# Attention by pairs of heads, and a new spread of the adaLN slots, in a two-layer encoder

## The chip, the cores and the metric

One core of a Trainium2 chip runs the whole program. The metric is the device time of one execution in microseconds (us); lower is better. Before the change the median of three runs is 1363.38 us (1358.85 to 1363.46).

## What is computed

Two sequences of 256 tokens (512 rows together) of width 1024 pass two encoder layers in fp32. A layer has two kinds of attention heads that read the same normalised input. Group A has 8 query heads of width 64 over 2 key/value heads, with a norm on each query and key and rotary positions. Group B has 8 heads whose queries (64 + 32 rotary columns) and keys/values are expanded from low-rank latents. Cut to what matters:

```python
mod = silu(c) @ w_ada[l] + b_ada[l]            # six vectors: shift/scale/gate, twice
h = rms_norm(x, g_attn) * (1 + scale_a) + shift_a
q_a, k_a, v_a, c_q, c_kv, k_r = split(h @ w_in)
o_a = softmax(rope(norm(q_a)) @ rope(norm(k_a)).T * 64**-0.5) @ v_a
q_b = rms_norm(c_q) @ w_uq                     # query expansion, 8 heads x 96
k_nope, v_b = split(rms_norm(c_kv) @ w_ukv)    # key/value expansion, 8 heads x (64 + 64)
o_b = softmax([q_b] @ [k_nope, rope(k_r)].T * 96**-0.5) @ v_b
x = x + gate_a * (concat(norm(o_a), norm(o_b)) @ w_o)
val, gate = split(conv3(norm_mod(x) @ w_up))
x = x + gate_f * ((silu(gate) * val) @ w_down)
```

## The kernel before, in words

The kernel writes each engine's program by hand; semaphores are the only order between engines. Weights come in **slots** of 128 x 1024 through a ring of four: SyncE (SP) loads a slot, ScalarE (ACT) rounds it to `w_hi` (L818), GpSimd (POOL) makes the rest `w_lo` (L446), and TensorE (PE) makes each product of three matmuls, hi x hi, hi x lo, lo x hi (`product`, L497 to L503). All matmul outputs lie in PSUM, eight banks of 512 columns.

Of `w_ada` all but the first vector is worked off on VectorE (DVE) in 88 **adaLN slots** of 128 x 1024: each is multiplied with silu(c) of either sequence and summed (`ada_slot`, L1038, both inputs in SBUF; or `ada_half_slot`, L1065, where half of silu(c) lies in PSUM, for vectors numbered `HALVED` and above). `ada_plan` is a table that says behind which step DVE takes a slot; `ADA_BEHIND` sets behind which weight slot SP queues its load.

A layer runs in these stages:

1. norm, then the input projection in five column chunks; DVE norms and rotates queries and keys (`QK_BLOCKS`, ends with L1237);
2. query expansion: 4 slots, each 4 row tiles x 2 x 3 matmuls of 192 columns; ACT copies the results to `qb` (L906); then key/value expansion: 2 slots, matmuls of 512 columns, copied to `kb` and `vb` (L913, L916);
3. attention over 32 **units** (`UNITS`), one head of one sequence each. For unit i PE transposes queries (and keys) into a bank (L663, L666, L667), ACT copies them out (`qa_t` L937, `qk_t` L939), PE makes the scores (L685), DVE takes the maximum (L1259) and its negative (L1262), ACT makes the exponentials with their sums (L949), PE transposes them (L693, two units late), DVE copies them out (L1268) and inverts the sum (L1269), PE multiplies with the values (L709, three units late), DVE divides (L1279). During the first scores PE runs 40 throw-away matmuls (`WARM_UP`, `keep_warm` L509). Between units DVE takes adaLN slots, 13 in layer 0 and none in layer 1;
4. transposes of the outputs (L540), output projection `w_o`, 8 tiles (`out_tile`), update of x (L1157) and its squares (L1144);
5. norm, then FFN in three groups of 8, 8 and 6 up tiles (ACT L993, DVE taps L1321, ACT silu L997, a_hi L999, DVE a_lo L1334) and 8 down tiles each.

`take` in `plan_banks` counts the uses of a bank, `wait_free` and `wait_full` are waits on them. POOL's rotation of `qb` and copy of the rotary keys (L466 to L475) come between two splits and end with `b_ready`.

## Time and profile before

| | us |
|---|---|
| median of 3 runs (lowest, highest) | 1363.38 (1358.85, 1363.46) |
| the profiled execution | 1359.79 |
| its span, first to last instruction | 1357.9 |
| mean granted TensorE clock | 0.959 |
| busy: PE, PE weight load | 1233.1 (91%), 1040.1 (77%) |
| busy: DVE, ACT, POOL | 819.2 (60%), 565.8 (42%), 470.1 (35%) |

A matmul's time is modelled from its start to its end and neighbours overlap, so a busy PE is not PE at its peak. Times of instructions below count from the start of the span. The program is long and its stages have different limits, so it is read stage by stage: the stage borders used are the start of the first query expansion, of the first scores, of the first `w_o` product, and of the sums for the next norm.

### The profile page before, as it was taken

Reading aid. Unit: us, or ns where it says so; the run is one execution under the profiler, and the core shown is the slowest. Engines: PE = TensorE matmul, PEld = TensorE weight load, DVE = VectorE, ACT = ScalarE, POOL = GpSimd, SP = SyncE. Lnnn points to the kernel's source line nnn. Section 1 sums busy time; section 2 is a strip of 40 time slices with the busy share of each in tenths; the row PEclk is TensorE's granted clock in tenths of the full one; section 3 lists DMA queues with packets and bytes.
Section 4 is the critical chain, followed back from the end, with each engine's and each line's share of the span. In section 5 each row is a group of like instructions: output and inputs, shape, how many; then the busy total and the mean of one; then the engine's idle time right before and its main releaser. Section 6 shows DMA issues by size and latency. Waiting matters only on the chain.

```text
span 1357.9 us, 19350 instructions
## 1 busy us (share of the span) xinstructions
PE 1233.1 (91%) x6424; PEld 1040.1 (77%) x6424; DVE 819.2 (60%) x1641; ACT 565.8 (42%) x1041; POOL 470.1 (35%) x224
## 2 busy tenths in 40 slices
PE   4798887795999999899978999999899999999996
PEld 0697776674788887778757998887778888888885
DVE  5668578777766667866865584764466513321444
ACT  1844445522644234223335546663454314432451
POOL 0244400032244433352453455003234543453452
PEclk9897979997999999899989989999999999999998
DMA  9433222033244634554542232001133331332221
GB/s 375 157 123 113 90 78 69 26 109 124 78 150 153 212 130 161 179 196 152 172 153 78 79 107 65 1 1 63 63 109 124 110 108 62 101 120 89 92 94 62
DMA packets 42748, 153.68 MB, mean 113 GB/s; under 512 B 4912, under 2 KB 5424, under 8 KB 42288
## 3 DMA queue, kind: packets, MB, share of 16 engines
q1 hardware_dynamic: 42672, 152.72, 32.7%
q8 instruction: 41, 0.67, 0.2%
q14 instruction: 35, 0.29, 0.1%
HBM read 150.61 MB, written 2.10 MB: 112 GB/s over the span
## 4 chain that ended last, share of the span: by engine, by line
issue 62%; POOLq 34%; PE 2%; POOL 1%; DVE 0%; DMA 0%; DVEq 0%; ACT 0%; SPq 0%; ACTq 0%
POOLq L447 33%; PE ps L497 1%; PE ps L503 1%; PE ps L498 1%; POOL qb_tmp L466 0%; POOL qb L471 0%; POOLq L452 0%; DMA c_all<-c_rows 0%; POOLq L476 0%; DVE x L1356 0%; POOLq L445 0%; POOLq L448 0%; PE ps L528 0%; POOL kb L473 0%; PE ps L523 0%
## 5 line engine op out<-in xcount | busy, mean ns | idle before, releaser
L446 POOL TENSOR_TENSOR w_lo<-w_raw,w_hi 128x1024 fp32r<-128x1024 f32 x184 | 450.0, 2446 | 859.7 <-ACT w_hi L818 835.3
L497 PE MATMUL ps<-h_hi,w_hi 128*128 128x512 f32 x832 | 329.8, 396 | 16.6 <-POOLq L448 7.9
L498 PE MATMUL ps<-h_lo,w_hi 128*128 128x512 f32 x832 | 325.6, 391 | 0.0
L503 PE MATMUL ps<-h_hi,w_lo 128*128 128x512 f32 x832 | 325.4, 391 | 0.0
L818 ACT CAST w_hi<-w_raw 128x1024 fp32r<-128x1024 f32 x184 | 187.2, 1047 | 140.6 <-PE ps L497 140.2
L1321 DVE SCALAR_TENSOR_TENSOR u_sb<-ps,par,u_sb 128x510 f32<-128x510 f32 x176 | 131.8, 749 | 122.6 <-ACT u_sb L993 110.1
L497 PEld LDWEIGHTS ps<-h_hi,w_hi 128*128 128x128 f32 x832 | 157.2, 189 | 61.9 <-issue 14.7
L503 PEld LDWEIGHTS ps<-h_hi,w_lo 128*128 128x128 f32 x832 | 157.2, 189 | 33.0
L498 PEld LDWEIGHTS ps<-h_lo,w_hi 128*128 128x128 f32 x832 | 157.4, 189 | 31.6
L1065 DVE SCALAR_TENSOR_TENSOR ada_prod<-ada_raw,ps 128x512 f32<-128x512 f32 x224 | 144.9, 684 | 8.6 <-issue 0.9
L497 PE MATMUL ps<-a_hi,w_hi 128*128 128x512 f32 x352 | 139.3, 396 | 11.0 <-DVEq L1159 7.5
L498 PE MATMUL ps<-a_lo,w_hi 128*128 128x512 f32 x352 | 138.6, 394 | 0.0
L503 PE MATMUL ps<-a_hi,w_lo 128*128 128x512 f32 x352 | 138.5, 394 | 0.0
L1157 DVE SCALAR_TENSOR_TENSOR x<-ps,mod,x 128x256 f32<-128x256 f32 x128 | 56.1, 480 | 136.1 <-PE ps L503 134.1
L993 ACT ACTIVATE u_sb<-ps,par 128x512 f32<-128x512 f32 x88 | 67.7, 775 | 146.8 <-PE ps L503 146.8
L1038 DVE SCALAR_TENSOR_TENSOR ada_prod<-ada_raw,c_all 128x1024 f32<-128x1024 f32 x64 | 92.4, 1443 | 8.7 <-DMA ada_raw<-ada_slots 3.7
L949 ACT ACTIVATE prob<-ps,nmx 128x256 f32<-128x256 f32 x128 | 59.5, 469 | 82.5 <-DVE nmx L1262 79.8
L497 PE MATMUL ps<-w_hi,h_hi 128*128 128x256 f32 (+1 forms) x320 | 91.3, 285 | 0.4 <-DVE h_lo L1109 0.3
L498 PE MATMUL ps<-w_lo,h_hi 128*128 128x256 f32 (+1 forms) x320 | 90.0, 281 | 0.0
L503 PE MATMUL ps<-w_hi,h_lo 128*128 128x256 f32 (+1 forms) x320 | 89.9, 281 | 0.0
L497 PEld LDWEIGHTS ps<-a_hi,w_hi 128*128 128x128 f32 x352 | 67.1, 191 | 28.0 <-POOLq L448 7.3
L997 ACT ACTIVATE sil<-u_sb 128x512 f32<-128x512 f32 x44 | 27.8, 633 | 126.6 <-DVEq L1326 126.6
(129 smaller groups left out, 1713.8 us busy)
## 6 DMA issues: line engine op xcount, KB each, us to landing
w_raw<-w_slots SPq DMA_DIRECT2D x184, 512.0 KB, 3.5
ada_raw<-ada_slots SPq DMA_DIRECT2D x88, 512.0 KB, 4.5
shift<-shift_slots SPq DMA_DIRECT2D x2, 2048.0 KB, 12.1
x<-x_t SPq DMA_DIRECT2D x2, 1024.0 KB, 12.8
y_t<-x SPq DMA_DIRECT2D x8, 256.0 KB, 2.2
c_all<-c_rows SPq DMA_DIRECT2D x1, 1024.0 KB, 5.1
par<-params SPq DMA_DIRECT2D x1, 251.0 KB, 10.7
tab<-tables SPq DMA_DIRECT2D x1, 192.0 KB, 10.0
```

Of the source, the lines that this page charges most:

```text
L446: nc.gpsimd.tensor_tensor(w_lo[:, j, :], w_raw[:, j, :], w_hi[:, j, :].bitcast(F32), ALU.subtract)
L447: nc.gpsimd.drain()
L497: hh = mm(out, stat[0], mov[0], start=first, stop=False)
L498: hl = mm(out, stat[0], mov[1], start=False, stop=False)
L503: return mm(out, stat[1], mov[0], start=False, stop=last)
L818: nc.scalar.copy(w_hi[:, j, :], w_raw[:, j, :]).then_inc(hi_done, 1)
L949: A(prob[:, i % 3, q, :], ps[:, i % 3, q * SEQ:(q + 1) * SEQ], ACT.Exp, bias=nmx[:, i, q:q + 1], scale=d ** -0.5, accum_out=sme[:, i, q:q ...
L993: A(u_sb[:, e, half, :], ps[:, bank(key), :], ACT.Identity, bias=par[:, L, bass.ds(ft + PC_CB, 1)], scale=par[:, L, bass.ds(ft + (PC_CW + ...
L1038: V.scalar_tensor_tensor(out=ada_prod[:], in0=ada_raw[:, j % 4, :], scalar=1.0, in1=c_all[:, s, :], op0=ALU.mult, op1=ALU.mult, accum_out= ...
L1065: V.scalar_tensor_tensor(out=ada_prod[:, 512 * s:512 * s + 512], in0=ada_raw[:, q % 4, 512 * t:512 * t + 512], scalar=1.0, in1=ps[:, 6 + s ...
L1157: V.scalar_tensor_tensor(out=xs, in0=ps[:, bank(key), c], scalar=gate, in1=xs, op0=ALU.mult, op1=ALU.add)
L1321: V.scalar_tensor_tensor(out=u3[:, :, dst:dst + SEQ - 1], in0=p3[:, :, src:src + SEQ - 1], scalar=par[:, L, bass.ds(at + (PC_CW + tap * 2 ...
```

## The change

- **Expansions.** Query heads are expanded by fours: 2 slots with matmuls of 384 columns in place of 4 with 192. Keys and values share one slot. Their expansion no longer stands ahead of the attention: the keys' half stands before the first scores and the values' half behind them. The warm-up matmuls of the attention go; those of the norms stay. A layer has 89 weight slots, not 92.
- **Pairs.** 32 units become 16 pairs: for group A heads p and p + 4, for group B heads h and h + 1, of one sequence. Scores of a pair fill two banks (two sets), one DVE instruction takes the negative maxima of both heads, ACT makes four exponentials without sums, ACT (not DVE) copies the transposed pair out in one instruction, and a column of ones behind the values (`va`, `vb`, 65 columns a head) gives the sums in the product with the values. The softmax scale moves into the query norm's weights and into the copy of `qb`. The exponentials are transposed one pair late, the values come two pairs late.
- **adaLN slots.** Layer 0: attention 13 to 16, `w_o` 8 to 5, FFN 48 to 40 (up tiles of the second group 15 to 11, of the third 11 to 7; up tiles with two slots go from 12 to 4). Layer 1: attention 0 to 8, up tiles of the first group 8 as before. Which vectors go in halves follows from that.

```diff
-S_UKV = S_UQ + 4
-S_WO = S_UKV + 2
+S_UKV = S_UQ + 2
+S_WO = S_UKV + 1
+PAIRS = [("a", s, (p, p + 4)) for s in range(NSEQ) for p in range(4)]
+PAIRS += [("b", s, (h, h + 1)) for s in range(NSEQ) for h in range(0, HEADS, 2)]
+S_BANK, PT_BANK, QT_BANK, O_BANK = (0, 2), 4, 6, 7
-HALVED = 4
+HALVED = (4, 5, 6, 7, 8, 10)
...
-    plan += [(("unit", i), S_WO - 1, 1) for i in range(1, 26, 2)]
-    plan += [(("wo", m), S_WO + m, 1) for m in range(KD)]
-    ups = [[1] * 8, [2, 2, 2, 2, 2, 2, 2, 1], [2, 2, 2, 2, 2, 1]]
+    plan += [(("unit", i), S_WO - 1, 1) for i in range(1, NP + 1)]
+    plan += [(("wo", m), S_WO + m, 1) for m in range(1, 6)]
+    ups = [[1] * 8, [1, 2, 1, 2, 1, 2, 1, 1], [2, 1, 1, 1, 1, 1]]
+    plan += [((1, "unit", i), SLOTS + S_WO - 1, 1) for i in range(1, KD + 1)]
...
-WARM_UP = {-1: 14, 0: 12, 1: 8, 2: 6}
-STATS_AT_UNIT = {12: (0, 0), 20: (0, 1), 28: (1, 0)}
+STATS_AT_STEP = {6: (0, 0), 10: (0, 1), 14: (1, 0)}
...
+                def expand_kv(s):
+                    j = slot(L, S_UKV)
+                    pe.wait_ge(ct_ready, 3 * L + 3)
                     for t in range(TT):
+                        key = ("ukv", s, t)
+                        wait_free(pe, L, key)
+                        product(ps[:, bank(key), :], [r[:, 2, t * P:t * P + P] for r in (ct_hi, ct_lo)],
+                                [r[:, j, s * 512:s * 512 + 512] for r in (w_hi, w_lo)], True, True,
...
+                def fill(j, part):
+                    pe.wait_ge(qt_ready, n)
...
+                def scores(j):
+                    pe.wait_ge(qt_ready, FILLS * L + fills_before(j + 1))
...
+                        pe.wait_ge(exp_ready, 4 * (NP * L + j - 1))
...
+                def prob_transposes(j):
+                    pe.wait_ge(pt_ready, NP * L + j)
+                    for u in range(2):
                         for q in range(2):
+                            pe.wait_ge(exp_ready, 4 * (NP * L + j) + 2 * u + q + 1)
...
+                def outputs(j):
+                    pe.wait_ge(o_done, NP * L + j)
+                    pe.wait_ge(pt_ready, NP * L + j + 1)
...
+                for i in range(-1, NP + 2):
+                    if i + 1 < NP:
+                        fill(i + 1, 0)
+                    if i == -1:
+                        expand_kv(0)
+                    if 0 <= i < NP:
+                        scores(i)
+                    if i == 0:
+                        expand_kv(1)
+                    if i + 1 < NP and PAIRS[i + 1][0] == "b":
+                        fill(i + 1, 1)
+                    if 0 <= i - 1 < NP:
+                        prob_transposes(i - 1)
+                    if 0 <= i - 2 < NP:
+                        outputs(i - 2)
+                    if i >= NP:
+                        for k in range(2):
+                            output_transposes(L, 2 * (i - NP) + k)
...
+                for i in range(-1, NP + 1):
+                    if i + 1 < NP:
+                        if i + 1 >= 2:
+                            act.wait_ge(s_full, NP * L + i)
+                        take_fill(i + 1, 0)
+                    if i + 1 < NP and PAIRS[i + 1][0] == "b":
+                        take_fill(i + 1, 1)
+                    if 0 <= i - 1 < NP:
+                        j = i - 1
+                        act.wait_ge(pt_full, NP * L + j + 1)
...
+                        nc.scalar.copy(prob_t[:, j % 2, :, :, :],
+                                       ps[:, PT_BANK:PT_BANK + 2, :].rearrange("p u (k q) -> p u k q", k=2)
+                                       ).then_inc(pt_ready, 1)
...
+                    if 0 <= i < NP:
+                        act.wait_ge(max_ready, NP * L + i + 1)
+                        for c in range(4):
+                            A(prob[:, i % 2, c, :], ps[:, S_BANK[i % 2] + c // 2, (c % 2) * SEQ:(c % 2 + 1) * SEQ],
+                              ACT.Exp, bias=nmx[:, i, c:c + 1]).then_inc(exp_ready, 1)
...
+                for k in range(KD // 2):
                     output_hi(L, k)
+                act.wait_ge(o_done, NP * (L + 1))
                 stats(1, 1)
...
+                for i in range(NP + 2):
+                    if i < NP:
+                        b = S_BANK[i % 2]
+                        dve.wait_ge(s_full, NP * L + i + 1)
+                        V.tensor_reduce(out=nmx[:, i, :], in_=ps[:, b:b + 2, :].rearrange("p u (q k) -> p (u q) k", q=2),
+                                        op=ALU.max, axis=AX_X, negate=True).then_inc(max_ready, 1)
...
+                        V.reciprocal(r4, o4[:, :, :, HD:VW])
...
+                            V.tensor_tensor(o_sb[:, 2 * s:2 * s + 2, col:col + HD], o4[:, u, :, 0:HD],
+                                            r4[:, u].broadcast_to([P, 2, HD]), ALU.mult)
```

How the rows stand on PE at the start of the attention of layer 0 (`proj` holds queries and keys of group A, `prob` the exponentials). Before, from the key transposes on:

```order
L652 MATMUL ps<-ident,proj 128x128 x4
L663 MATMUL ps<-ident,proj 128x128 x2
L509 MATMUL ps<-ones 128x128 x26
L685 MATMUL ps<-ka_t,qa_t 128x256 x2
L663 MATMUL ps<-ident,proj 128x128 x2
L509 MATMUL ps<-ones 128x128 x8
L685 MATMUL ps<-ka_t,qa_t 128x256 x2
L509 MATMUL ps<-ones 128x128 x6
```

Now, from the end of the values' expansion on:

```order
L517 MATMUL ps<-w_hi,ct_lo 128x512
L680 MATMUL ps<-ident,proj 128x128 x2
L708 MATMUL ps<-ka_t,qk_t 128x256 x4
L722 MATMUL ps<-ident,prob 128x128 x8
L680 MATMUL ps<-ident,proj 128x128 x2
L708 MATMUL ps<-ka_t,qk_t 128x256 x4
L722 MATMUL ps<-ident,prob 128x128 x8
L738 MATMUL ps<-va,prob_t 128x65 x8
```

The throw-away matmuls are gone, and one row now holds the scores, transposes or value products of two heads; a pair has as many matmuls as two units had.

On DVE in the attention of layer 0, one unit with a slot before, and what follows it:

```order
L1259 TENSOR_REDUCE mx<-ps 128x2
L1262 TENSOR_SCALAR nmx<-mx 128x2
L1268 COPY prob_t<-ps 128x512
L1269 RECIPROCAL rin<-sme 128x2
L1279 TENSOR_TENSOR o_sb<-ps,rin 128x2x64
L1038 SCALAR_TENSOR_TENSOR ada_prod,mod<-ada_raw,c_all 128x1024 x2
```

Now, a whole pair between two slots:

```order
L1101 SCALAR_TENSOR_TENSOR ada_prod,mod<-ada_raw,c_all 128x1024 x2
L1324 TENSOR_REDUCE nmx<-ps 128x4
L1332 RECIPROCAL rin<-ps 128x4
L1336 TENSOR_TENSOR o_sb<-ps,rin 128x2x64 x2
L1101 SCALAR_TENSOR_TENSOR ada_prod,mod<-ada_raw,c_all 128x1024 x2
```

The copies of the transposed exponentials and the negations have left DVE, and a slot comes with every pair instead of with every second unit.

On DVE at the end of the output projection of layer 0, before, from the update of x for the last tile to the reciprocal of the next norm:

```order
L1157 SCALAR_TENSOR_TENSOR x<-ps,mod,x 128x256 x2
L1144 TENSOR_TENSOR ssum<-ssum,sq_x 128x512
L1038 SCALAR_TENSOR_TENSOR ada_prod,mod<-ada_raw,c_all 128x1024 x2
L1080 TENSOR_TENSOR mod<-mod,par 128x16
L1084 TENSOR_SCALAR mod<-mod 128x16
L1086 TENSOR_TENSOR mod<-mod,par 128x16
L1144 TENSOR_TENSOR ssum<-ssum,sq_x 128x512
L1094 RECIPROCAL rstd<-root 128x4
```

Now, from the last slot (behind tile 5) to the same reciprocal:

```order
L1101 SCALAR_TENSOR_TENSOR ada_prod,mod<-ada_raw,c_all 128x1024 x2
L1143 TENSOR_TENSOR mod<-mod,par 128x16
L1147 TENSOR_SCALAR mod<-mod 128x16
L1149 TENSOR_TENSOR mod<-mod,par 128x16
L1220 SCALAR_TENSOR_TENSOR x<-ps,mod,x 128x256 x2
L1207 TENSOR_TENSOR ssum<-ssum,sq_x 128x512
L1220 SCALAR_TENSOR_TENSOR x<-ps,mod,x 128x256 x2
L1207 TENSOR_TENSOR ssum<-ssum,sq_x 128x512 x2
L1157 RECIPROCAL rstd<-root 128x4
```

The slot and the finishing of its vector have moved from between the last update of x and the norm to two tiles ahead of it.

## Rows read from the trace of the kernel before

**Rows 1.** Windows between stage borders: borders, length, busy time (count) by engine, clock, DMA.

```profile
117.14:147.06 29.92, 28.03 (x179) 26.81 (x180) 13.54 (x21) 18.05 (x37) 21.51 (x18) 0.79 0.45 159
147.06:264.38 117.32, 94.22 (x636) 83.87 (x635) 93.21 (x221) 57.17 (x178) 5.39 (x7) 0.93 0.18 59
264.38:331.71 67.33, 49.46 (x211) 38.26 (x209) 53.05 (x72) 17.74 (x27) 21.47 (x8) 0.89 0.35 118
331.71:731.59 399.88, 378.59 (x1628) 308.22 (x1628) 273.56 (x620) 147.12 (x193) 164.72 (x68) 0.97 0.45 154
801.70:827.12 25.42, 25.42 (x175) 24.21 (x174) 10.38 (x17) 18.04 (x37) 20.77 (x16) 0.87 0.45 146
827.12:918.25 91.13, 85.62 (x637) 78.92 (x635) 63.87 (x167) 57.18 (x178) 6.16 (x9) 0.98 0.01 1
918.25:971.47 53.22, 47.06 (x212) 37.28 (x210) 20.89 (x37) 17.73 (x27) 19.25 (x8) 1.00 0.24 80
971.47:1345.18 373.71, 368.71 (x1629) 302.96 (x1629) 159.90 (x276) 144.36 (x190) 156.32 (x65) 1.00 0.28 92
```

**Rows 2.** Waits of PE, 147 to 262 us: us in total, times, longest.

```profile
PE ps L693 <- DVEq L1270: 18.2, 12, 2.2
PE ps L685 <- ACTq L941: 4.9, 4, 2.4
```

**Rows 3.** Waits of PE, 332 to 745 us: us in total, times, longest.

```profile
PE ps L523 <- DVEq L1146: 15.5, 2, 12.7
PE ps L497 <- POOLq L448: 9.8, 7, 3.8
PE ps L497 <- DVEq L1159: 7.5, 3, 5.7
```

**Rows 4.** Timeline of DVE at the end of L1237: start, us.

```profile
129.22 2.60 DVE L1237 TENSOR_TENSOR proj<-proj,st_qk 128x512 f32<-128x512 f32 x1
810.04 2.61 DVE L1237 TENSOR_TENSOR proj<-proj,st_qk 128x512 f32<-128x512 f32 x1
```

**Rows 5.** Timeline of PE in layer 1: scores of neighbouring units, group A (two apart), group B.

```profile
843.92 1.03 PE L685 MATMUL ps<-ka_t,qa_t 128*128 128x256 f32 x4
848.49 1.03 PE L685 MATMUL ps<-ka_t,qa_t 128*128 128x256 f32 x4
...
902.32 1.03 PE L685 MATMUL ps<-qk_t 96*128 96x256 f32 x4
904.90 1.03 PE L685 MATMUL ps<-qk_t 96*128 96x256 f32 x4
```

**Rows 6.** Groups by line, engine and shape: busy us, mean ns, idle before.

```profile
L1214 DVE TENSOR_REDUCE st_qk<-sq_qk 128x16 f32<-128x1024 f32 x4 | 4.9, 1221 | 1.0 <-ACT sq_qk L886 0.8
L1269 DVE RECIPROCAL rin<-sme 128x2 f32<-128x2 f32 x64 | 9.9, 155 | 0.0
L1279 DVE TENSOR_TENSOR o_sb<-ps,rin 128x128 f32<-128x128 f32 x64 | 18.7, 292 | 16.5 <-issue 12.3 <-PE ps L709 4.2
L949 ACT ACTIVATE prob<-ps,nmx 128x256 f32<-128x256 f32 x128 | 59.5, 469 | 82.5 <-DVE nmx L1262 79.8 <-issue 2.6
L818 ACT CAST w_hi<-w_raw 128x1024 fp32r<-128x1024 f32 x184 | 187.2, 1047 | 140.6 <-PE ps L497 140.2 <-issue 0.3
L939 ACT COPY qk_t<-ps 96x512 f32<-96x512 f32 x32 | 18.6, 580 | 7.8 <-issue 6.0 <-PE ps L667 1.5
```

**Rows 7.** Timeline of DVE in the attention of layer 0: a slot, and the next unit's maximum.

```profile
210.97 1.22 DVE L1038 SCALAR_TENSOR_TENSOR ada_prod<-ada_raw,c_all 128x1024 f32<-128x1024 f32 x1
...
213.63 0.69 DVE L1259 TENSOR_REDUCE mx<-ps 128x2 f32<-128x512 f32 x1
```

**Rows 8.** Timeline of DVE in the output projection of layer 0: two updates of x, half a slot.

```profile
305.68 0.88 DVE L1157 SCALAR_TENSOR_TENSOR x<-ps,mod,x 128x256 f32<-128x256 f32 x2
...
308.91 3.24 DVE L1038 SCALAR_TENSOR_TENSOR ada_prod<-ada_raw,c_all 128x1024 f32<-128x1024 f32 x1
...
312.29 0.88 DVE L1157 SCALAR_TENSOR_TENSOR x<-ps,mod,x 128x256 f32<-128x256 f32 x2
```

More of the change, by code:

```diff
@@ L82 @@
 SLOTS = _at
-ROUNDS = SLOTS // RING
-assert SLOTS % RING == 0 and sum(GROUPS) == FT
+assert sum(GROUPS) == FT
 PC_GATTN = 0
@@ L177, in plan_banks @@
         take(("lat", j), 4 + j)
-    for s in range(4):
+    for s in range(2):
         for t in range(TT):
@@ L182, in plan_banks @@
         for t in range(TT):
-            take(("ukv", s, t), t)
+            take(("ukv", s, t), 4 + t % 2)
     take("kat", 7)
-    pairs = 0
-    for i in range(-1, NU + LAG_O):
-        if i + 1 < NU and UNITS[i + 1][3]:
-            take(("qt", i + 1), 4 + pairs % 2)
-            pairs += 1
-        if 0 <= i < NU:
-            take(("s", i), i % 3)
-        if 0 <= i - LAG_P < NU:
-            take(("pt", i - LAG_P), 3)
-        if 0 <= i - LAG_O < NU:
-            take(("o", i - LAG_O), 6 + (i - LAG_O) % 2)
     for k in range(KD):
@@ L262, in encoder_kernel @@
         kr_rot = put("kr_rot", [P, TT, ROT])
+        at_cg = base[0]
         cg = put("cg", [P, 2, 2, HD])
@@ L626, in _ @@
                             last.then_inc(full[t], 1)
-                width = 2 * QK_B
-                for s in range(4):
+                width = 4 * QK_B
+                for s in range(2):
                     j = slot(L, S_UQ + s)
@@ new lines, in scores @@
+                def scores(j):
+                    group, s, heads = PAIRS[j]
+                    pe.wait_ge(qt_ready, FILLS * L + fills_before(j + 1))
+                    if j == 0:
+                        pe.wait_ge(ka_ready, L + 1)
+                    if j < 2:
+                        for t in range(S_BANK[j], S_BANK[j] + 2):
+                            key = ("uq", 1, t)
+                            pe.wait_ge(free[bank(key)], n_use(L, key) + 1)
+                    else:
+                        pe.wait_ge(exp_ready, 4 * (NP * L + j - 1))
+                    for u in range(2):
@@ new lines, in scores @@
+                    last.then_inc(s_full, 1)
+                def prob_transposes(j):
+                    if j == 0:
+                        for t in range(2, TT):
+                            key = ("ukv", 1, t)
+                            pe.wait_ge(free[bank(key)], n_use(L, key) + 1)
+                    pe.wait_ge(pt_ready, NP * L + j)
+                    for u in range(2):
+                        for q in range(2):
+                            pe.wait_ge(exp_ready, 4 * (NP * L + j) + 2 * u + q + 1)
+                            for k in range(2):
+                                last = nc.tensor.transpose(ps[:, PT_BANK + u, k * SEQ + q * P:k * SEQ + q * P + P],
+                                                           prob[:, j % 2, 2 * u + q, k * P:k * P + P], ident[:])
+                    last.then_inc(pt_full, 1)
@@ L712, in _ @@
-                    if i >= NU:
-                        output_transposes(L, i - NU)
-                for k in range(LAG_O, KD // 2):
-                    output_transposes(L, k)
+                                v = va[:, 2 * s + k, u, :] if group == "a" else vb[:, 2 * s + k, heads[u], :]
+                                c = (2 * u + q) * VW
+                                last = mm(ps[:, O_BANK, c:c + VW], prob_t[:, j % 2, u, k, q * P:q * P + P], v,
+                                          start=(k == 0), stop=(k == 1))
@@ new lines, in outputs @@
+                    last.then_inc(o_full, 1)
+                for i in range(-1, NP + 2):
[14 more added lines that the diff above has]
+                    if i >= NP:
+                        for k in range(2):
+                            output_transposes(L, 2 * (i - NP) + k)
@@ L1415, in _pack @@
     halved = ada.reshape(-1, KD // 2, 2, P, 2, SLOT // 2).transpose(0, 4, 1, 3, 2, 5).copy()
-    for n in range(HALVED, len(ORDER)):
+    for n in HALVED:
         for q in range(KD):
```

346 lines of the change are left out of this document (148 added, 198 removed).

## The prediction

> **What bounds the kernel now.** I read the windows between stage borders first, because a share over the whole span mixes stages with different limits, then PE's waits in the stages where PE has idle time, then the instructions behind those waits. The layers do the same work except for adaLN slots, so the same stage of the other layer is the best yardstick. Three things are to be seen [rows 1]:
>
> - Attention, first scores to first `w_o` product, takes 117.3 us in layer 0 and 91.1 in layer 1. In layer 1 PE is busy 85.6 of 91.1; it is the limit there. In layer 0 PE is busy only 94.2 of 117.3 and DVE 93.2. PE waits 18.2 us for bank 3, which DVE frees late (L1270), and 4.9 for the query copies of ACT [rows 2]; the clock falls to 0.93. This stage waits on DVE with its 13 slots.
> - The output projection takes 67.3 us in layer 0 and 53.2 in layer 1. PE waits 12.7 us once for the sums of the norm [rows 3], which DVE ends behind 8 slots.
> - The FFN takes 399.9 us in layer 0 (48 slots) and 373.7 in layer 1 (8 slots). Waits of 9.8 us for splits and 7.5 for banks [rows 3] are layer 0's.
>
> Between the norm's sums and the first expansion I expect no difference, and none in the prologue.
>
> **Part 1: expansions ahead of the attention.** The stage from the first query expansion to the first scores takes 29.9 and 25.4 us with PE hardly idle [rows 1]. Now the key transposes need the query expansion and DVE's norm of the keys. The latter ends at 131.8 and 812.7 us [rows 4], 14.7 us after the first expansion in layer 0 and 11.0 in layer 1. The expansion is 48 matmuls of 384 columns, 18432 columns: 15.4 us at 1.2 GHz and 7.7 at 2.4. PE starts it at 1.2 GHz after a pause (granted 0.79 and 0.87 in these windows, and 1.00 later [rows 1]). So layer 0 waits for DVE, 14.7 us; in layer 1 the expansion ends last or nearly so, 12.3. From there to the first scores PE has 8 transposes and the keys' expansion, 12 matmuls of 512 columns: 7168 columns or 3.0 us at 2.4 GHz. ACT must have copied `ka_t`, the first queries and a first bank of keys meanwhile, so some 1.6 us of waiting: 4.6 (bounds 3.0, and 9 if ACT's copies lie bare). The stage becomes 19.3 and 16.9 us: **-10.6 and -8.5**. The 40 warm-up matmuls a layer are inside this sum and the next.
>
> What comes along costs nothing on the path. Three weight slots a layer less is 3 x 1.05 us less on ACT [rows 6], with as many splits and loads. The copy of the values in two pieces, one scaling of the query weights and four small memsets on POOL lie beside PE; POOL's rotation (`b_ready`) is needed only at pair 8, some 30 us later. On SP 16 loads now queue behind weight slot `S_WO` + 6 and hold the next one until the attention is over; that slot is needed at the last `w_o` tile, over 35 us later.
>
> **Part 2: pairs.** PE's work in a pair is that of two units. At full clock neighbouring units start 2.58 us apart in group B and two units 4.57 us apart in group A [rows 5], so a pair costs 5.16 and 4.57, and 16 pairs 8 x 9.73 = 77.8 us. One more column for each head is noise. The values' expansion adds 6144 columns, 2.6 us: PE needs 80.4.
>
> DVE per pair: maximum over 1024 columns 1.22, reciprocal 0.16, two products 0.58 [rows 6] and a slot, 2.66 from its start to the next instruction [rows 7]: 4.62 and some drains, about 4.8. That is under 5.16 and a little over 4.57. ACT per pair in group B: four exponentials of at most 0.47, two fills of 0.58 and one copy of 1024 columns, at most 1.05 (nearest row L818) [rows 6]: 4.1. In group A it is less. No engine is above PE's 77.8 by much, so PE should be the limit with slots or without.
>
> Waits remain, since each engine is in order. ACT's copy of `prob_t` now stands ahead of the next exponentials and waits for PE; PE's next `fill` waits until ACT has emptied the one bank for queries, and scores queue behind it; three times ACT squares outputs between pairs; at the end the last pair's maximum, exponentials, copy and products lie bare. The bounds are none, and the 23.1 us that PE idles in layer 0's old stage (5.5 in layer 1) [rows 1]. I take 5.3 for layer 1, near its old 5.5, and 8.5 for layer 0, as its slots fill DVE. With 2.3 us from the last product over the division to the first `w_o` product, the stage takes 80.4 + 8.5 + 2.4 = 91.3 in layer 0, **-26.0**, and 80.4 + 5.3 + 2.3 = 88.0 in layer 1, **-3.1**.
>
> **Part 3: output projection.** In layer 1 PE idles 6.2 of 53.2 us [rows 1]. Part of it is the fourth output tile, whose remainder on DVE stood behind the norm of group B; now the first four all come before it. I take **-2.6** (bounds 0 and -6.2). In layer 0 DVE needs 6.61 us per tile with a slot, 3.24 of it one half that runs beside a split on POOL [rows 8], and a PE tile of 24 x 512 columns takes 5.1. Eight such tiles are 12.7 us late at the norm; five slots, behind tiles 1 to 5, put DVE up to 7.5 late, and two tiles without slots (under 2 us each) give most of it back. So layer 0 comes to layer 1's 50.6 and half a us more: 67.3 to 51.1, **-16.2**.
>
> **Part 4: FFN of layer 0.** It is 26.2 us longer than layer 1's, and layer 1 takes 8 single slots without loss. Up tiles with two slots go from 12 to 4 and no two are neighbours; by their number alone 26.2 x 8/12 = 17 us come back. Lateness also no longer adds up from tile to tile, so I take **-20** (bounds -4 and -26).
>
> **Sum.** 10.6 + 8.5 + 26.0 + 3.1 + 2.6 + 16.2 + 20 = 87.0 us. Against the profiled execution, 1359.8 us (span 1357.9), that is 1272.8. The profiled one lies 3.6 under the median, so I round up: **1275 us**.
>
> **Rivals.**
>
> - *Exchange between ACT and PE sets the pair.* With exponentials at 0.47 apiece, ACT does 1.9 of exponentials and 0.8 of the first fill, PE fills again (0.4) and transposes (0.9), ACT copies (1.05); with half a us for semaphores 5.5 us a pair in group B, 5.0 in group A: 84 a layer and not 77.8, or 13 us in both, 1288; if ACT's squares all lie bare as well, 1294. For it: one bank for fills. Against: before, PE waited only 4.9 us for fills. Chance 0.15.
> - *Slots and POOL in each other's way.* A slot in the attention takes 2.66 us [rows 7], but half a slot beside a split on POOL took 3.24 instead of 1.22 [rows 8]. Pairs 1 to 3 now run while POOL still splits one slot and rotates `qb`. Two us for the split and up to 0.5 for each other half make 4 us a layer on DVE, of which PE feels most in group A: 1282. Chance 0.1. The Trainium skill, SBUF — State Buffer, "Who interferes with whom", states it as a rule: a DVE instruction with two SBUF inputs contends with a GpSimd instruction that reads SBUF, and the later one waits in full. By that rule, vector 9, which goes from halves in PSUM to whole slots, loses a protection too. The trace agrees with the rule in the 3.24 against 1.22.
> - *The FFN keeps its waits.* Lateness there runs from taps over silu and cast to the next split, so a single two-slot tile may still hold PE. Then 4 us come back and not 20: 1291. Chance 0.1.
> - *Slower.* The matmuls that fell away kept PE busy. If PE ran at 1.2 GHz through both attentions, its 80.4 us would double: 161 less the waits it would cover (14), 1275 + 147 = 1422. It decides from more than half of the stage at the low level: 88 us of gain against 2 x 80.4. Against it: layer 1 held 0.98 with the same mixture, and layer 0 held 0.93 with 20% idle [rows 1]. Chance 0.04.
>
> **How the numbers follow.** The forecast has 0.61, with 1262 to 1286 by its own bounds (nothing waits in the attention, all 26 come back; or 3 us more in each of four stages). The first three rivals lie between 1282 and 1294, and two of them together give 1306. The range is 1260 to 1306. About 0.5% (7 us) is what a measurement tells from no change. All cases but the last are faster by far more: faster 0.96, same 0.01, slower 0.03.
>
> **What would show it.** Right: first scores some 10 and 8 us sooner; distances between scores of 5.2 us in group B and 4.6 to 4.9 in group A at clock 1.00 in both layers; PE's wait for the norm sums in layer 0 near 3 us instead of 12.7; both FFNs within 8 us of each other. Wrong: distances over 5.5 us, waits of PE for ACT at each fill (exchange) or of DVE for POOL (slots); a clock under 0.9 in the attention; FFN waits for splits near 10 us as before. A total above 1306 would mean that pairs are slower than two units.

## The result, and the profile after

The change makes the kernel faster: 1291.69 us median (1291.19 to 1293.44) against 1362.26 for the kernel before in the same session, ratio 0.9488 (95% interval 0.9467 to 0.9509). That is 70.6 us; 87 were forecast. The time lies inside the range of 1260 to 1306, but outside the forecast's own bounds of 1262 to 1286, among the times of the rivals. The profiled execution took 1291.37 us, its span 1289.3, at a mean granted clock of 0.971.

The windows between the same stage borders in the changed kernel answer to [rows 1] (borders, length, busy time and count by engine, clock, DMA), with expansions, attention, projection and FFN of layer 0, then of layer 1:

```profile
117.01:136.19 19.18, 15.53 (x69) 14.01 (x70) 13.57 (x21) 11.00 (x21) 7.46 (x3) 0.85 0.38 138
136.19:234.77 98.58, 88.85 (x618) 81.16 (x617) 72.93 (x137) 68.88 (x140) 16.09 (x22) 0.95 0.28 88
234.77:292.15 57.38, 47.94 (x209) 37.05 (x209) 46.24 (x60) 15.82 (x23) 20.32 (x8) 0.98 0.36 118
292.15:674.27 382.12, 371.95 (x1629) 306.43 (x1629) 255.18 (x552) 147.66 (x193) 163.82 (x68) 0.98 0.44 150
743.88:760.42 16.54, 14.20 (x68) 12.98 (x69) 11.15 (x17) 11.22 (x21) 7.51 (x3) 0.90 0.30 97
760.42:852.12 91.70, 85.90 (x619) 78.64 (x617) 53.19 (x104) 67.76 (x138) 16.09 (x22) 0.98 0.16 53
852.12:902.81 50.69, 47.39 (x208) 37.19 (x208) 21.23 (x37) 16.43 (x25) 19.22 (x8) 1.00 0.26 84
902.81:1276.51 373.70, 368.72 (x1629) 302.98 (x1629) 160.13 (x276) 144.37 (x190) 156.30 (x65) 1.00 0.28 92
```

| stage, us | before | forecast | after | off by |
|---|---|---|---|---|
| expansions, layer 0 / 1 | 29.9 / 25.4 | 19.3 / 16.9 | 19.2 / 16.5 | -0.1 / -0.4 |
| attention, layer 0 / 1 | 117.3 / 91.1 | 91.3 / 88.0 | 98.6 / 91.7 | +7.3 / +3.7 |
| output projection, layer 0 / 1 | 67.3 / 53.2 | 51.1 / 50.6 | 57.4 / 50.7 | +6.3 / +0.1 |
| FFN, layer 0 / 1 | 399.9 / 373.7 | 379.9 / 373.7 | 382.1 / 373.7 | +2.2 / 0 |

So nearly all that is missing lies in the two attentions (11.0 us) and in the output projection of layer 0 (6.3). One border of the kernel before was read wrong: the 801.70 of [rows 1] lies 0.7 us behind the start of layer 1's first query expansion, which is at 800.99, so that stage took 26.1 us and not 25.4.

The waits of PE from the first scores of layer 0 to the first query expansion of layer 1 (136 to 745 us; total, times, longest) answer to [rows 2, 3]:

```profile
PE ps L537 <- DVEq L1209: 10.4, 2, 7.2
PE ps L684 <- ACTq L988: 6.9, 3, 2.7
PE ps L511 <- DVEq L1222: 5.8, 3, 5.0
...
PE ps L722 <- ACT prob L1014: 1.1, 1, 1.1
PE ps L511 <- POOLq L461: 0.3, 1, 0.3
```

The 18.2 us for bank 3 are gone, and so are the FFN's waits for splits, 9.8 us before and 0.3 now. The wait for the norm's sums (L537) is 7.2 us, not near 3. The second line is most of what is left in the attention (4.9 us for query copies before): PE cannot refill the one query bank (L684) until ACT has emptied it (L988).

PE in the attention of layer 0, scores of neighbouring pairs (L708) and the longest waits, which answer to [rows 5] (start, length, instruction, idle time before):

```profile
148.74 1.89 PE L708 MATMUL ps<-ka_t,qk_t 128*128 128x256 f32 x8
...
153.31 1.89 PE L708 MATMUL ps<-ka_t,qk_t 128*128 128x256 f32 x8
...
171.79 0.31 PE L684 MATMUL ps<-ident,qb 128*96 128x128 f32 x1 [2.70 <-ACTq L988]
...
185.74 1.89 PE L708 MATMUL ps<-qk_t 96*128 96x256 f32 x8
...
190.95 1.89 PE L708 MATMUL ps<-qk_t 96*128 96x256 f32 x8
195.47 0.45 PE L684 MATMUL ps<-ident,qb 128*96 128x128 f32 x1 [2.62 <-ACTq L988]
...
202.22 3.15 PE L708 MATMUL ps<-qk_t 96*128 96x256 f32 x8
...
208.69 1.89 PE L708 MATMUL ps<-qk_t 96*128 96x256 f32 x8
```

Undisturbed pairs are 4.57 and 5.21 us apart, as forecast (4.57 and 5.16). But the scores at 202.22 come 11.27 us after those at 190.95. 2.62 us of the excess is a wait; the rest is the clock, as the windows of PE there show (PE's busy time, clock, DMA):

```profile
192.00:196.00 4.00, 1.38 (x7) 0.81 0.18 40
196.00:200.00 4.00, 4.00 (x21) 0.50 0.23 93
200.00:204.00 4.00, 4.00 (x17) 0.50 0.00 0
204.00:208.00 4.00, 4.00 (x31) 0.91 0.40 130
```

PE stood still for 2.6 us, and the granted clock then went to 0.50, the lower level. It costs 11.27 - 5.21 - 2.62 = 3.4 us in this distance and 6.47 - 5.21 = 1.3 in the next: 4.7. The same happens once in layer 1 (a wait of 2.22 at 819.04; distances of 9.28 and 5.53): 2.2 us.

What ACT did before the wait of 2.62 us in layer 0:

```profile
190.30 1.57 ACT L1014 ACTIVATE prob<-ps,nmx 128x256 f32<-128x256 f32 x4 [0.31 <-DVE nmx L1324]
191.74 0.65 ACT L872 ACTIVATE junk_o<-o_sb 128x512 f32<-128x512 f32 x1
...
192.55 0.63 ACT L872 ACTIVATE junk_o<-o_sb 128x512 f32<-128x512 f32 x1
...
193.33 1.28 ACT L878 ACT_TABLE_LOAD   x1
...
194.83 0.56 ACT L986 COPY qk_t<-ps 96x512 f32<-96x512 f32 x1
...
199.33 1.28 ACT L1014 ACT_TABLE_LOAD   x1
```

Behind pair 10 two squares (L872), the square root for the norm of group A (L878) and a load of the function table stand between the exponentials and the copy that frees the query bank; a second table load stands ahead of the next exponentials. The first wait (2.70) follows the squares behind pair 6, whose exponentials had also waited 1.61 us for a maximum that DVE made late. The third (1.62, at 217.41) has no squares ahead of it. There DVE takes a slot and its norm of group A (`NORM_A_AT`, four products) ahead of the maximum of pair 13, and the exponentials wait for it; DVE, then ACT:

```profile
212.25 1.68 DVE L1191 TENSOR_SCALAR o_sb<-o_sb,st_o 128x512 f32<-128x512 f32 x4
214.05 1.23 DVE L1324 TENSOR_REDUCE nmx<-ps 128x4 f32<-128x1024 f32 x1
...
215.31 1.57 ACT L1014 ACTIVATE prob<-ps,nmx 128x256 f32<-128x256 f32 x4 [2.37 <-DVE nmx L1324]
```

In the kernel before, the squares and the root stood in the attention too, and the root held PE there already. These are PE's scores behind its copy of queries, in layer 0 and in layer 1:

```profile
226.46 1.10 PE L685 MATMUL ps<-qk_t 96*128 96x256 f32 x4 [2.39 <-ACTq L941]
...
884.06 1.94 PE L685 MATMUL ps<-qk_t 96*128 96x256 f32 x4 [1.79 <-ACTq L941]
```

Undisturbed scores take 1.03 us [rows 5]. Behind the second of these waits they took 1.94, at a granted clock of 0.57 (884 to 888 us); behind the first the clock stayed at 1.00.

DVE in the output projection of layer 0 answers to [rows 8]:

```profile
264.96 0.88 DVE L1220 SCALAR_TENSOR_TENSOR x<-ps,mod,x 128x256 f32<-128x256 f32 x2
...
268.19 3.24 DVE L1101 SCALAR_TENSOR_TENSOR ada_prod<-ada_raw,c_all 128x1024 f32<-128x1024 f32 x1
...
271.57 0.88 DVE L1220 SCALAR_TENSOR_TENSOR x<-ps,mod,x 128x256 f32<-128x256 f32 x2
...
285.59 0.88 DVE L1220 SCALAR_TENSOR_TENSOR x<-ps,mod,x 128x256 f32<-128x256 f32 x2
...
288.59 3.38 DVE L1207 TENSOR_TENSOR ssum<-ssum,sq_x 128x512 f32<-128x512 f32 x2 [0.21 <-issue]
```

A tile with a slot still takes 6.61 us. The last output tile on PE ends at 284.9 (292.15 less the wait of 7.24), and only at 285.59 does DVE come to the update of the second last one. Of the last two sums of squares (the last row) one took 2.57 us and the other 0.69; the long one ran beside a split on POOL (288.27 to 290.61). Both of its inputs lie in SBUF.

### The profile page after: what moved, and what is told of

It reads as the page before. It is cut to its first block, busy times and chain, and to the rows that moved or that the text cites. A ratio compares the mean times of both kernels' runs of the same rounds, so it can differ in the third digit from the quotient of the medians.

```text
span 1289.3 us, 17964 instructions
## 1 busy us (share of the span) xinstructions
PE 1196.3 (93%) x6168; PEld 1009.3 (78%) x6168; DVE 764.4 (59%) x1416; ACT 572.3 (44%) x931; POOL 461.6 (36%) x227
## 4 chain that ended last, share of the span: by engine, by line
issue 60%; POOLq 35%; PE 2%; POOL 2%; DVE 1%; DMA 0%; DVEq 0%; ACT 0%; SPq 0%; ACTq 0%
POOLq L460 33%; PE ps L511 1%; PE ps L517 1%; PE ps L512 1%; POOL qb L485 1%; POOL kb L488 1%; POOLq L491 0%; POOL qb_tmp L480 0%; POOLq L466 0%; DMA c_all<-c_rows 0%; DVE x L1414 0%; POOLq L458 0%; POOLq L461 0%; PE ps L542 0%; PE ps L537 0%
## 5 line engine op out<-in xcount | busy, mean ns | idle before, releaser
L459 POOL TENSOR_TENSOR w_lo<-w_raw,w_hi 128x1024 fp32r<-128x1024 f32 x178 | 433.7, 2437 | 799.2 <-ACT w_hi L862 772.3
L862 ACT CAST w_hi<-w_raw 128x1024 fp32r<-128x1024 f32 x178 | 180.9, 1047 | 142.5 <-PE ps L511 142.2
L1128 DVE SCALAR_TENSOR_TENSOR ada_prod<-ada_raw,ps 128x512 f32<-128x512 f32 x192 | 124.2, 684 | 6.4
L1101 DVE SCALAR_TENSOR_TENSOR ada_prod<-ada_raw,c_all 128x1024 f32<-128x1024 f32 x80 | 111.8, 1397 | 10.9 <-DMA ada_raw<-ada_slots 3.6
L511 PE MATMUL ps<-w_hi,h_hi 128*128 128x256 f32 (+1 forms) x320 | 91.5, 286 | 0.1
L517 PEld LDWEIGHTS ps<-a_hi,w_lo 128*128 128x128 f32 x352 | 66.5, 189 | 14.0
L512 PEld LDWEIGHTS ps<-a_lo,w_hi 128*128 128x128 f32 x352 | 66.5, 189 | 13.7
```

The source lines that it names most:

```text
L459: nc.gpsimd.tensor_tensor(w_lo[:, j, :], w_raw[:, j, :], w_hi[:, j, :].bitcast(F32), ALU.subtract)
L511: hh = mm(out, stat[0], mov[0], start=first, stop=False)
L512: hl = mm(out, stat[0], mov[1], start=False, stop=False)
L517: return mm(out, stat[1], mov[0], start=False, stop=last)
L862: nc.scalar.copy(w_hi[:, j, :], w_raw[:, j, :]).then_inc(hi_done, 1)
L1101: V.scalar_tensor_tensor(out=ada_prod[:], in0=ada_raw[:, j % 4, :], scalar=1.0, in1=c_all[:, s, :], op0=ALU.mult, op1=ALU.mult, accum_out= ...
```

## Experiments

The theory after this reading: PE sets the pair, slots fit beside it, and the missing gain is ACT's squares with the root in the attention, and whole slots beside POOL's splits in the projection. The first rival is that the spread of the slots made the gain and pairs little; the second that slots hold up DVE in the attention whatever ACT does. All times are medians; ratios are against the kernel before on the same chip. The after kernel stands at 1291.69, 0.9488.

### Slots alone

The kernel before with the new table:

```diff
-    plan += [(("unit", i), S_WO - 1, 1) for i in range(1, 26, 2)]
-    plan += [(("wo", m), S_WO + m, 1) for m in range(KD)]
-    ups = [[1] * 8, [2, 2, 2, 2, 2, 2, 2, 1], [2, 2, 2, 2, 2, 1]]
+    plan += [(("unit", i), S_WO - 1, 1) for i in range(1, 33, 2)]
+    plan += [(("wo", m), S_WO + m, 1) for m in range(1, 6)]
+    ups = [[1] * 8, [1, 2, 1, 2, 1, 2, 1, 1], [2, 1, 1, 1, 1, 1]]
+    plan += [((1, "unit", i), SLOTS + S_WO - 1, 1) for i in range(1, 16, 2)]
```

> The kernel before with the new spread of the adaLN slots alone (16 behind units of layer 0, 5 behind output tiles, 40 in its FFN, 8 behind units of layer 1). Theory (units leave DVE no room, pairs do): output projection of layer 0 falls from 67.3 to about 57 us, its FFN from 400 to 382, but its attention grows by three slots of 2.66 us, 117 to 125, and layer 1's by some 4: 1346 us in all. Rival (the spread is what made the gain, pairs little): 1310 or less, with the attention of layer 0 no longer than 117.

Measured: 1361.38 us, ratio 0.9994 (0.9975 to 1.0013): no gain. Windows of attention, projection and FFN of layer 0, and of layer 1's attention:

```profile
147.56:268.66 121.10, 99.00 (x636) 86.50 (x635) 99.96 (x233) 57.16 (x178) 5.31 (x7) 0.89 0.21 70
268.66:329.55 60.89, 49.18 (x212) 38.26 (x210) 45.63 (x60) 17.72 (x27) 20.41 (x8) 0.94 0.32 106
329.55:708.37 378.82, 371.67 (x1629) 304.88 (x1629) 248.32 (x550) 147.37 (x193) 164.94 (x68) 0.99 0.43 151
805.35:915.29 109.94, 93.84 (x636) 84.19 (x635) 82.71 (x202) 57.17 (x178) 6.33 (x9) 0.92 0.12 39
```

Projection and FFN give 27.5 us, as expected, but eight slots among layer 1's units cost 18.8 us (91.1 to 109.9), 2.35 each, nearly their length, and layer 0's attention grew by 3.8. The expectation's "some 4" for layer 1 was wrong: between units there is next to no room. The rival falls: the spread by itself is worth nothing.

### Pairs alone

The changed kernel with the old table (13, 8 and 48 slots in layer 0, none in layer 1's attention; vector 9 in halves again), the lines above the other way round.

> The changed kernel with the old spread of slots (13 behind pairs of layer 0, 8 behind output tiles, 48 in its FFN, none in layer 1's attention). Theory: both attentions stay within 3 us of the changed kernel's 98.6 and 91.7, output projection of layer 0 goes back from 57.4 to about 67 and its FFN from 382 to 400: 1319 us. Rival (the spread is what freed the attention): the attention of layer 0 is back over 110 and the whole at 1335 or more.

Measured: 1310.18 us, ratio 0.9623 (0.9607 to 0.9639). Windows of the two attentions:

```profile
136.27:232.21 95.94, 87.38 (x619) 79.93 (x617) 65.61 (x125) 68.05 (x138) 16.09 (x22) 0.96 0.24 78
781.23:870.08 88.85, 84.22 (x618) 77.09 (x617) 33.01 (x71) 67.09 (x138) 12.42 (x22) 1.00 0.02 7
```

So pairs, with the expansions, give 52 us of the 70.6. No run has the expansions alone; by the stages some 20 of the 52 lie in them. The output projection took 63.3 (67 expected) and the FFN 398.7, whose waits for splits are back at 11.3 us. The spread gives 18.5 us on top of pairs and nothing clear of noise without: layer 1's attention takes eight slots for 2.85 us (88.85 to 91.70), 0.36 each, where units paid 2.35.

### No slots in the attention

```diff
-                    ada_at(L, ("unit", i))
+                    for _ in range(ADA_TAKES.get((L, "unit", i), 0)):
+                        n, q = taken[0] // KD, taken[0] % KD
+                        dve.wait_ge(ada_landed[q % 4], 16 * (2 * n + q // 4 + 1))
+                        dve.sem_inc(ada_used, 1)
...
+                        taken[0] += 1
```

> The changed kernel without DVE's multiplications of the 24 slots that stand in the two attentions (their vectors are left out of the computation; loads and order stay). Theory (a pair lasts as long as PE needs, slots fit beside it): distances between scores stay 4.56 and 5.21 us, only the last two pairs of layer 0, where a slot stands ahead of the last maximum and the last division, get shorter by 2 to 3 us: 1289. Rival (slots and POOL or PSUM readers get in each other's way): both attentions get shorter by 4 us or more, 1283 or less.

Measured: 1278.2 us, ratio 0.939 (0.9375 to 0.9406). The rival's number came, though layer 1 got shorter by 2.9 us and not by 4. Its two attentions:

```profile
136.49:225.37 88.88, 84.23 (x618) 77.10 (x617) 33.35 (x73) 67.12 (x138) 12.42 (x22) 1.00 0.30 101
750.32:839.17 88.85, 84.21 (x619) 77.08 (x617) 33.18 (x72) 67.10 (x138) 12.42 (x22) 1.00 0.17 54
```

Distances between undisturbed pairs stay at 4.57 and 5.21, so it is not POOL or PSUM that slots get in the way of. The waits for fills behind the squares of pairs 6 and 10 shrink from 2.70 and 2.62 to 0.80 and 2.22, the one behind DVE's norm (1.62) is gone, one of 0.57 stands behind the second table load, and the clock stays at 1.00. So 16 slots cost 9.7 us in layer 0 and 8 cost 2.85 in layer 1, not in the steady pairs but at those waits. This calls for the counterpart.

### No squares in the attention

```diff
-                        stats(g, s)
                         if (g, s) == (0, NSEQ - 1):
-                            group_root(0)
+                            act.sem_inc(o_root, 1)
```

> The changed kernel without ACT's squares and root between the pairs (the sums of squares of group A, and of the first sequence of group B, are left out of the computation; slots stay). Theory (neither slots nor squares hold PE by themselves, only a square behind a late maximum does): waits for fills under 1 us, clock at its upper level, attention 89 us in layer 0 and 87.5 in layer 1: 1278. Rival (slots alone make DVE late): the attention of layer 0 stays over 95: 1288 or more.

Measured: 1279.02 us, ratio 0.9385 (0.9367 to 0.9404). Its two attentions:

```profile
138.36:230.11 91.75, 86.98 (x618) 80.32 (x617) 72.90 (x137) 61.59 (x123) 16.08 (x22) 0.96 0.30 95
755.25:840.92 85.67, 83.88 (x618) 77.21 (x617) 53.13 (x104) 60.75 (x123) 16.08 (x22) 1.00 0.18 56
```

Layer 1, us in its attention: slots without squares 85.67, squares without slots 88.85, both 91.70. Eight slots by themselves leave PE 1.8 us of waits, so its own work is 83.9 us in a layer. Layer 0 came to 91.75, not 89: waits of 1.04, 1.60 and 1.06 us remain and the clock fell near its end, so 16 slots do cost something by themselves. The 1.60 is the wait behind DVE's norm of group A, unchanged, which confirms that squares have no part in it. In layer 0 the changed kernel lies 14.7 us over 83.9; without slots 9.7 come back, without squares 6.8, together more than there is (in layer 1 2.9 and 6.0 of 7.8). So a part of the cost belongs to both: squares behind a maximum that slots made late, and the clock that falls after a wait. The wait behind pair 6 in layer 0 shows it: 1.04 us with slots alone, 0.80 with squares alone, 2.70 with both. Neither single cause is enough. Without slots 88.9 us are left in either layer, 5.0 over PE's own work, and 3.6 of it are the waits of 0.80, 2.22 and 0.57 behind squares, root and table load.

### Values' expansion ahead of the scores

```diff
                     if i == -1:
                         expand_kv(0)
+                        expand_kv(1)
...
-                    if i == 0:
-                        expand_kv(1)
```

> The changed kernel with the values' half of the key/value expansion ahead of the first scores too, and no throw-away matmuls. Theory: first scores 2.6 us later and the attention as much shorter, but the first maximum (1.23) and the first exponentials (1.57) now have only one pair's scores beside them: PE waits some 3 us, 1295. Rival (the clock needs the matmuls there): the granted clock falls to its lower level after the first scores in both layers and each attention loses 5 us, 1302. Second rival (nothing hangs on the place): 1292.

Measured: 1299.5 us, ratio 0.9536 (0.9519 to 0.9552); 7.8 us slower than the change. The expansions became 4.0 and 3.4 us longer (23.2 and 19.9), and the attention did not become shorter (102.7 and 92.0). Without those 12 matmuls of 512 columns among the first scores new waits appear, 1.46 and 1.45 us for exponentials a few pairs later, and in layer 0 the stage's clock is 0.92 (0.95 in the change). In layer 1 it is 0.96 (0.98). The theory's direction held with too small a price; how much of it is the clock was not taken apart.

### The root at the end, and the squares one by one

The root behind the last exponentials, and with it DVE's norm of group A at the end and ahead of the slot there; then also one row tile of squares at a step:

```diff
-STATS_AT_STEP = {6: (0, 0), 10: (0, 1), 14: (1, 0)}
-NORM_A_AT = 12
+STATS_AT_STEP = {6: (0, 0), 7: (0, 1), 9: (0, 2), 10: (0, 3), 13: (1, 0), 14: (1, 1)}
+NORM_A_AT = NP
...
-                        if (g, s) == (0, NSEQ - 1):
-                            group_root(0)
+                    if i == NP - 1:
+                        group_root(0)
```

> The changed kernel with the square root for the norm of group A behind the last exponentials (it stands in the middle of them, behind pair 10, and brings two loads of ACT's function table of 1.28 us each), and DVE's norm of group A in the second last step. Theory (this root holds ACT back, PE's fills stand still for it and the clock falls): PE's waits for fills lose their longest one, the clock stays at its upper level in the second half, attention of layer 0 from 98.6 to 92 us and of layer 1 from 91.7 to 89: 1282. Rival (the squares, 1.7 us at a step, are enough to hold PE): under 2 us gained in each, 1289. Rival (the root now lies bare at the end): 1292 or more.

> As the run with the late root, and the squares of the outputs one row tile at a step (pairs 6, 7, 9, 10, 13, 14) in place of two at one step (6, 10, 14). Theory (what ACT does between two pairs is hidden as long as it is under a microsecond): no wait of PE for a fill over 1 us is left, attention 90 us in layer 0 and 87 in layer 1: 1278. Rival (six steps with 0.85 us wait as long together as three with 1.7): as the late root alone.

Measured: 1294.61 us, ratio 0.9501 (0.9463 to 0.954), and 1295.31, 0.9516 (0.9481 to 0.9551): neither is faster than the change. The waits inside did nearly what was expected: with both edits layer 0 has 1.90, 0.42 and 0.41 us where it had 2.70, 2.62 and 1.62 (the last of these went with DVE's norm, not with the squares). But at the end stands a new one; PE in the run with both (the first lies at the fill for pair 8, the last ahead of the output transposes):

```profile
171.86 0.32 PE L684 MATMUL ps<-ident,qb 128*96 128x128 f32 x1 [1.90 <-ACTq L988]
...
224.81 1.97 PE L554 MATMUL ps<-ident,o_sb 128*128 128x128 f32 x8 [2.93 <-DVEq L1192]
```

The transposes take 1.97 in place of 1.04 us: the clock has fallen again (0.50 from 226 to 230 us), and stays low into the output projection (clock 0.95 and 0.96 there in layers 0 and 1, 0.98 and 1.00 in the change). The attention took 95.0 and 93.3 us with both, 98.8 and 93.6 with the late root alone: shorter than in the change only in layer 0 and with both edits, longer in layer 1. The wait was moved, not removed. That root and squares were the cause by themselves was wrong; the rival of the bare end was right.

### Slots earlier

```diff
-    plan += [(("unit", i), S_WO - 1, 1) for i in range(1, NP + 1)]
-    plan += [(("wo", m), S_WO + m, 1) for m in range(1, 6)]
+    plan += [(("unit", i), S_WO - 1, 2 if i == 0 else 1) for i in range(NP + 1)]
+    plan += [(("wo", m), S_WO + m, 1) for m in range(1, 4)]
```

> The changed kernel with two adaLN slots more in layer 0's attention, both behind the first maximum, where DVE waits 6.8 us for the second pair's scores, and three slots behind output tiles (1 to 3) in place of five. Theory (DVE behind slots beside a split sets the end of the output projection): its stage falls from 57.4 to 51.5 us, attention as before: 1286. Rival (the place behind the first maximum is not free, since the weights' split on POOL and the next maximum are due there): attention 3 us longer or more, 1289 or over.

> The late root, the squares one by one and the earlier slots together. Theory (three separate causes): the gains add up, attention 90 and 87, output projection 51.5 in layer 0: 1272. Rival (one cause behind them, lateness of DVE that only moves): less than two thirds of the sum of the single gains.

Measured: 1290.66 us, ratio 0.9478 (0.9444 to 0.9512), and 1290.07, 0.947 (0.9435 to 0.9505) with the two edits above: both as the change within the interval. The projection fell to 53.1, with the wait for the norm's sums back at layer 1's 2.8, but the attention grew to 101.0: behind the first maximum two slots are one too many (PE waits 1.55 us for the exponentials of the next pair). The sum of gains did not come, since the single gains did not.

### The end covered

Squares one by one and the late root, the last products ahead of the output transposes, one slot behind the first maximum, and layer 1's slots in steps 0 and 8 to 14; beside it the root by itself behind pair 11:

```diff
-                    if i >= NP:
-                        for k in range(2):
-                            output_transposes(L, 2 * (i - NP) + k)
+                    if i > NP:
+                        for k in range(4):
+                            output_transposes(L, k)
```

> Squares one by one and the late root as before, but PE makes the last products with the values ahead of the first output transposes, which waited 2.93 us for the root; slots of layer 0 start behind the first maximum (17 in the attention, 4 behind output tiles), those of layer 1 stand in steps 0 and 8 to 14. Theory: the last products cover most of the 2.93 us, the clock stays up there, attention 92.5 in layer 0 and 88 in layer 1, output projection 55: 1279. Rival (the end is bare in any order, since the last products wait for the same ACT): attention as in the run with root and squares, 95 and 93, 1288.

> As the run before with squares one by one and the same slots, but the root of group A in the middle, by itself behind pair 11, and the output transposes where the change has them. Theory (root and its two table loads, 2.9 us at one step, hold PE once per layer by some 2 us, and cost less than at the end): attention 95 in layer 0 and 89 in layer 1, output projection 55: 1284. Rival (a slot in the steps of group B costs more than one in group A): layer 1 at 92 or more.

Measured: 1283.86 us, ratio 0.9418 (0.94 to 0.9437), and 1285.92, 0.9441 (0.9418 to 0.9464). Both intervals lie below the change's, the second only just, so the first is faster than the change and the second may be. The wait of 2.93 us is gone from both its layers and 0.87 stands in its place. Attention took 96.2 and 89.4 us (97.0 and 91.2 with the root in the middle, where PE waits 0.97 and 0.56 us for fills behind the root and its second load, and then 2.00 behind DVE's norm of group A, which that run left in the middle too). So layer 1 came near its forecast of 88 and layer 0 did not: 17 slots there still make a maximum late (ACT waits up to 2.88 us for one), and behind a wait of 1.06 us near the end the granted clock lay at 0.50 from 222 to 230 us. The run changes four things at once; what each is worth was not taken apart.

### Halves behind the output tiles

The first of these two runs, with all slots of vector 3 behind the eight output tiles, as halves; the edit is against the change:

```diff
-HALVED = (4, 5, 6, 7, 8, 10)
+HALVED = (3, 4, 5, 6, 7, 8, 10)
-    plan += [(("unit", i), S_WO - 1, 1) for i in range(1, NP + 1)]
-    plan += [(("wo", m), S_WO + m, 1) for m in range(1, 6)]
+    plan += [(("unit", i), S_WO - 1, 1) for i in (0, 1, 2, 3, 4, 6, 8, 9, 10, 11, 12, 13, 14)]
+    plan += [(("wo", m), S_WO + m, 1) for m in range(KD)]
```

> As the run with the late root behind the last products, but all eight slots of one vector stand behind the output tiles of layer 0, as halves with silu(c) in PSUM, and 13 whole slots are left in its attention (steps 0 to 4, 6 and 8 to 14). Theory (behind an output tile it is the second SBUF operand beside POOL's split that makes one multiplication 3.24 us): halves take 0.75 us or less each, a tile with a slot 5.0 us of DVE in place of 6.6, and the output projection with eight slots takes 52.5 us where eight whole slots took 63.3 and four 53.8; attention of layer 0 about 93, 1280 in all. Rival (a slot costs the output projection 2 us in any form): 62 us there, 1290.

Measured: 1280.83 us, ratio 0.9417 (0.9401 to 0.9434): the lowest of the runs that compute everything, not to be told from the run with the end covered. DVE and POOL behind an output tile (the update, two of the four products of one slot, the next update; the split that ran beside the two):

```profile
246.33 0.88 DVE L1220 SCALAR_TENSOR_TENSOR x<-ps,mod,x 128x256 f32<-128x256 f32 x2
...
249.62 0.69 DVE L1128 SCALAR_TENSOR_TENSOR ada_prod<-ada_raw,ps 128x512 f32<-128x512 f32 x1
...
250.23 0.68 DVE L1128 SCALAR_TENSOR_TENSOR ada_prod<-ada_raw,ps 128x512 f32<-128x512 f32 x1
...
251.05 0.88 DVE L1220 SCALAR_TENSOR_TENSOR x<-ps,mod,x 128x256 f32<-128x256 f32 x2
...
249.01 2.40 POOL L459 TENSOR_TENSOR w_lo<-w_raw,w_hi 128x1024 fp32r<-128x1024 f32 x1 [3.23 <-ACT w_hi L862]
```

The two products that ran beside the split at 249.01 took 0.69 and 0.68, as those outside it, and the split 2.40; from update to update it is 4.72 us, not 6.61. The stage took 54.6 us with eight slots. With whole slots and pairs it took 63.3 (eight), 57.4 (five), 54.9 (four) and 53.1 (three): about 2 us a slot. PE still waits 7.0 us for the sums, since the eighth slot (277.98 to 281.74 with its finish) stands between the last update and the last sum; DVE's copies of silu(c) into PSUM, 2.6 us in all, come on top of the slots. Attention of layer 0, with 13 slots, came to 91.5.

## Why the prediction was right, and where it was not

- **Part 1** held in its sum: 19.2 and 16.5 us against 19.3 and 16.9. Layer 0 waited for DVE's norm of the keys, as forecast. In layer 1 the number came by luck: the expansion took 10.2 us and not 12.3, since PE was at its lower clock for some 3.5 us only, and PE then waited 1.67 us for DVE's norm, which ended 11.7 us after the first expansion. The 11.0 of the forecast was counted from the border that lies 0.7 us late. That the values' expansion stands among the first scores is worth 7.8 us, as the run with it ahead shows; the prediction counted nothing for it.
- **Part 2** had the pair right: 4.57 and 5.21 apart, and DVE needs 4.76 us for a pair with a slot (5.21 less 0.45 of idle time). In the run with slots alone two units with one slot kept it 6.77 us (from the maximum at 841.62 to the one at 848.39): this is the room that pairs made. PE's work was 83.9 with the end included, where 80.4 + 2.4 stood, 1.1 us short. The waits, 8.5 and 5.3, were nearly right: 9.7 us in layer 0 and 5.7 in layer 1. They had been chosen between bounds and not added up from single waits, so that is luck in part. **What failed is the step from a wait to its price**: each was counted for its length alone. The granted clock fell to its lower level behind one of them in either layer and cost another 4.7 and 2.2 us. The kernel before showed this too, in layer 1 behind the root (scores of 1.94 in place of 1.03 us at 884.06). 83.9 + 9.7 + 4.7 = 98.3 and 83.9 + 5.7 + 2.2 = 91.8, against 98.6 and 91.7 measured.
- It also put layer 1's eight slots at nothing and layer 0's sixteen at 3.2 us; the runs show 2.9 and 9.7. In layer 1 most of it needs the squares behind a late maximum (without squares one wait of 0.72 us for a fill is left there); in layer 0 the slots, and with them DVE's norm of group A ahead of a maximum, also hold PE alone (3.7 us of waits without squares, and the lower clock behind the last). The prediction named the squares ("three times ACT squares outputs between pairs") but not the root between them with its two table loads, nor DVE's norm. The root could have been read in the kernel before: the 2.4 us that [rows 2] gives as the longest wait for query copies is the wait behind it.
- **Part 3** was right for layer 1 (50.7; the wait of 2.87 us for a remainder on DVE, at 923.58 before, is gone) and failed for layer 0 at "two tiles without slots give most of it back". Five slots made DVE late as computed, but two tiles only give time back while PE is still making tiles. It had made its last one before DVE reached the second last; their updates, squares and sums lay bare, 6.4 us in place of the "under 2 us each", 1.9 of it one sum beside POOL's split, and PE waited 7.2 us.
- **Part 4** was about right: 17.8 us, the 17 of the count, not 20. A wait of 5.0 us at a down tile is left. The rival that the FFN keeps its waits is excluded: waits for splits 9.8 before, 0.3 after, 11.3 with the old table.
- **The rivals.** The exchange between ACT and PE does not set the pair in steady state, but at two steps with squares and behind DVE's norm it does; that mixture of forecast and first rival is what came, at 1291.7. Slots and POOL: in the attention the longest product took 1.67 us against a median of 1.23, so little of the kind there; behind `w_o` it costs what was counted. The Trainium skill, SBUF — State Buffer, "Who interferes with whom", states the rule for two SBUF inputs; the traces agree: 3.24 us with both in SBUF beside a split (from 268.19 to 271.43, where the split ended at 270.35) and 0.69 for half as many elements with one in PSUM. That PE would run at 1.2 GHz throughout is excluded, the stages held 0.95 and 0.98; in small, behind single waits, the mechanism was there.

## What to carry to other kernels

When the limit of a stage moves from one engine to another, look up the small jobs of a third that held the new limit already: the root's wait of 2.39 us stood in the trace before, under DVE's 18.2, and with DVE's waits gone such waits were what was left. Price a wait of the matrix engine with the slow matmuls behind it, and look at lateness where the producer stops, not on the average of tiles. And try a spread of side work together with the change that makes room for it: it gave nothing clear of noise alone and 18.5 us with pairs.

## What the runs showed that was not expected

- Behind a wait of 2.62 us in layer 0 and of 2.22 in layer 1 the granted clock went to 0.50; behind a wait of 2.22 at the same step, without slots, it stayed at 1.00 in both layers, and with the root at the end it fell behind 2.93. With pairs alone the two long waits of layer 0 were as in the change, but the clock fell to 0.50 behind the first (2.69) and stayed at 1.00 behind the second (2.62), the other way round. Without squares it fell behind a wait of 1.06 us that left it at 1.00 in the change. So the length of one wait does not decide it alone; what else does was not settled.
